# Per-head products of a recurrent mixer moved between its projections, TensorE's layer loop written out

## The reference, cut to what matters

```python
x = x + 0.5 * swiglu_ffn(rmsnorm_2(x, norm_ffn1[l]), ffn1_w_up[l], ffn1_w_down[l])
x = x + hybrid_mixer(rmsnorm_2(x, norm_mix[l]), ...)
x = x + 0.5 * swiglu_ffn(rmsnorm_2(x, norm_ffn2[l]), ffn2_w_up[l], ffn2_w_down[l])
```

```python
proj = h @ w_in
u_pool, u_lru, u_gelu, g_logits = split(proj)            # 512, 1280, 1280, 2048 columns
pooled = trailing means over 2, 4, 8, 16 tokens - u_pool # 4 groups of 128
y_pool = ((pooled @ w_grp + b_grp) * scale) @ w_pool_up  # 4 per-head products 128x128
v = causal_conv(u_lru)                                   # 4 taps, 10 heads of 128
r = sigmoid(v @ w_a + b_a); i = sigmoid(v @ w_x + b_x)   # 20 per-head products 128x128
h = scan of a * h + sqrt(1 - a*a) * i * v, a = exp(-8 * r * softplus(-lam))
y_lru = (h * gelu(u_gelu)) @ w_lru_up
out = (sigmoid(g) halves: g_pool * y_pool + g_lru * y_lru) @ w_out
```

## Time and profile before

| | us |
|---|---|
| median of three runs | 2370.72 |
| the profiled execution | 2372.06 |
| its span, first to last instruction | 2370.3 |
| TensorE matmul busy | 2053.2 (87%) |
| VectorE busy | 890.1 (38%) |
| ACT busy | 735.4 (31%) |
| GpSimd busy | 27.8 (1%) |

### The profile page before, as it was taken

One profiled execution on the slowest core, in us unless ns is written; L12 is line 12 of the kernel. 1 busy time (PEld: TensorE's weight loads), 2 busy tenths in 40 slices (PEclk: granted clock), 3 DMA queues, 4 the chain that ended last, 5 costly groups with the idle time before them and its releaser, 6 DMA issues.

```text
span 2370.3 us, 35013 instructions
## 1 busy us (share of the span) xinstructions
PE 2053.2 (87%) x14775; PEld 1616.1 (68%) x14776; DVE 890.1 (38%) x1006; ACT 735.4 (31%) x796; POOL 27.8 (1%) x27
## 2 busy tenths in 40 slices
PE   7988867777777777777699998999999999899999
PEld 5858423333333333233399998999999999899999
DVE  5452100000000000000355576775555556677555
ACT  3442100000000000000143447554434443745443
POOL 0000000000000000000000001000000000100000
PEclk8997788887787878878799999999999999999999
DMA  9756699999999999999945664465574565446554
GB/s 328 286 188 248 255 429 429 429 428 428 429 428 429 429 429 429 428 429 428 366 143 156 182 205 143 146 228 178 143 228 150 166 185 189 167 136 213 178 156 130
DMA packets 235212, 657.34 MB, mean 277 GB/s; under 512 B 6932, under 2 KB 121940, under 8 KB 210516
## 3 DMA queue, kind: packets, MB, share of 16 engines
q1 hardware_dynamic: 235092, 655.62, 72.5%
HBM read 654.54 MB, written 1.05 MB: 277 GB/s over the span
## 4 chain that ended last, share of the span: by engine, by line
issue 61%; PE 38%; DVE 0%; POOL 0%; ACT 0%; DVEq 0%; POOLq 0%; ACTq 0%
PE psum L1085 12%; PE psum L1086 12%; PE psum L1087 12%; PE psum L1109 1%; PE psum L1111 1%; PE psum L1110 1%; PE psum L1149 0%; DVE work_r L2065 0%; POOL work L694 0%; DVE work L1983 0%; ACT ring_r L1382 0%; PE psum L1191 0%; PE psum L1190 0%; PE psum L1051 0%; POOL work L695 0%
## 5 line engine op out<-in xcount | busy, mean ns | idle before, releaser
L1085 PE MATMUL psum<-work_r,ring_r 128*128 128x256 f32 x2912 | 825.2, 283 | 4.2 <-DVE work_r L2065 4.2
L1087 PE MATMUL psum<-work_r,ring_r 128*128 128x256 f32 x2912 | 824.1, 283 | 0.0
L1085 PEld LDWEIGHTS psum<-work_r,ring_r 128*128 128x128 f32 x2912 | 558.8, 192 | 5.2 <-issue 4.6
L1087 PEld LDWEIGHTS psum<-work_r,ring_r 128*128 128x128 f32 x2912 | 559.0, 192 | 0.0
L1086 PE MATMUL psum<-h_lo,ring_r 128*128 128x256 f32 x1856 | 525.2, 283 | 0.0
L1846 DVE TENSOR_TENSOR ring_r<-ring,ring_r 128x2048 fp32r<-128x2048 f32 (+2 forms) x182 | 446.1, 2483 | 175.4 <-ACT ring_r L1382 174.7
L1382 ACT CAST ring_r<-ring 128x2048 fp32r<-128x2048 f32 (+2 forms) x180 | 359.6, 2035 | 369.3 <-PE psum L1087 346.7
L1086 PEld LDWEIGHTS psum<-h_lo,ring_r 128*128 128x128 f32 x1856 | 356.3, 192 | 0.1
L1086 PE MATMUL psum<-work_r,ring_r 128*128 128x256 f32 x1056 | 299.3, 283 | 0.0
L998 PE MATMUL psum<-ring,work 128*32 128x512 f32 x1536 | 215.4, 716 | 43.3 <-DMA ring<-in_w_up_e_dram 41.5
L1020 PE MATMUL psum<-ring,work 128*32 128x512 f32 x768 | 128.5, 804 | 89.2 <-DMA ring<-in_w_down_e_dram 89.2
(11 more groups left out here) (284 smaller groups left out, 1964.6 us busy)
## 6 DMA issues: line engine op xcount, KB each, us to landing
ring<-in_w_gate_e_dram SPq DMA_DIRECT2D x64, 2048.0 KB, 12.1
ring<-in_w_down_e_dram SPq DMA_DIRECT2D x48, 2048.0 KB, 31.6
ring<-in_ffn_w_up_dram SPq DMA_DIRECT2D x41, 2048.0 KB, 8.0
ring<-in_w_up_e_dram SPq DMA_DIRECT2D x32, 2048.0 KB, 21.4
work<-in_w_up_e_dram SPq DMA_DIRECT2D x32, 2048.0 KB, 30.1
ring<-in_w_in_dram SPq DMA_DIRECT2D x26, 2048.0 KB, 8.0
ring<-in_ffn_w_down_dram SPq DMA_DIRECT2D x32, 1408.0 KB, 7.0
work<-in_w_down_e_dram SPq DMA_DIRECT2D x16, 2048.0 KB, 37.2
```

The source lines that it names most:

```text
L1085: pe.matmul(out_b, w_hi[:, k, cols], hi[:, tokens], start=(k == 0), stop=False)
L1087: mm = pe.matmul(out_b, w_lo[:, k, cols], hi[:, tokens], start=False, stop=(k == n_k - 1))
```

## The change

On TensorE the per-head products no longer stand in a row: `ra 0` to `ra 2` come between `pool 0` and `pool 1`, `ra 3`, `ra 4` and `ix 0` to `ix 3` behind `pool 1`, `ix 4` between `gelu 1` and `gelu 2`, and `pmix` behind `gelu 2`. The list of groups, and with it the banks, follows that order. ACT no longer casts `proj 4` ahead of `lru_input(4)`; its two units are cast between the gates, and all five `gelu` activations come after the tanh. VectorE makes the `lo` of `proj 4` in two pieces, one ahead of the pooled values and one behind, and empties `pmix` later. Behind the scan VectorE makes one unit of `pup`, then the pool remainder, and only then the second unit and the last two groups of `g`. TensorE's loop over the layers becomes a Python loop, so its instructions stand twice in the program; ACT, VectorE, GpSimd and SP keep their loops.

The list of groups, and TensorE's code (`recurrence_gates` and `input_gates` hold what stood in the two loops):

```diff
-    mixer += [(("pool", g), "dve") for g in range(2)]
-    mixer += [(("ra", g), "act") for g in range(5)] + [(("ix", g), "act") for g in range(5)]
-    mixer += [(("pmix", g), "dve") for g in range(2)] + [(("gelu", g), "dve") for g in range(1, 5)]
+    mixer += [(("pool", 0), "dve")] + [(("ra", g), "act") for g in range(3)] + [(("pool", 1), "dve")]
+    mixer += [(("ra", g), "act") for g in (3, 4)] + [(("ix", g), "act") for g in range(4)]
+    mixer += [(("gelu", 1), "dve"), (("ix", 4), "act"), (("gelu", 2), "dve")]
+    mixer += [(("pmix", g), "dve") for g in range(2)] + [(("gelu", g), "dve") for g in (3, 4)]
...
-            with pe.Fori(0, LAYERS) as l:
+            for l in range(LAYERS):
...
-                for q in range(2):
-                    project(("pool", q), ("proj", 0), q)
-
...
+                project(("pool", 0), ("proj", 0), 0)
+                w = tile("small", 2 * HEADS + POOLS, P)
+                for q in range(3):
+                    recurrence_gates(q)
+                project(("pool", 1), ("proj", 0), 1)
+                for q in (3, 4):
+                    recurrence_gates(q)
+                for q in range(4):
+                    input_gates(q)
+                project(("gelu", 1), ("proj", 4), 0)
+                input_gates(4)
+                project(("gelu", 2), ("proj", 4), 1)
                 pe.wait_ge(pooled_ready, l + 1)
                 for q in range(2):
                     per_head(("pmix", q), w, 2 * HEADS, pooled, (2 * q, 2 * q + 1))
-                for i in (4, 5):
-                    for q in range(2):
-                        project(("gelu", 1 + 2 * (i - 4) + q), ("proj", i), q)
+                for q in range(2):
+                    project(("gelu", 3 + q), ("proj", 5), q)
```

On ACT (`head_gates` is the old body of the loop over the gates):

```diff
-                split(("proj", 4), l)
                 lru_input(4)
-                gelu(0)
...
+                for g in range(3):
+                    head_gates("ra", rgate, lo["lru_b_a"], g)
+                split(("proj", 4), l, (0,))
+                for g in (3, 4):
+                    head_gates("ra", rgate, lo["lru_b_a"], g)
+                for g in range(4):
+                    head_gates("ix", igate, lo["lru_b_x"], g)
+                split(("proj", 4), l, (1,))
                 split(("proj", 5), l)
+                head_gates("ix", igate, lo["lru_b_x"], 4)
                 wait_emptied(("ra", 4))
...
-                gelu(1)
-                gelu(2)
                 split(("proj", 6), l)
...
-                gelu(3)
-                gelu(4)
+                for g in range(5):
+                    gelu(g)
```

On VectorE:

```diff
-                split(("proj", 4), l)
                 conv(4)
                 for g in range(2):
                     scaled(pool_u[:, 2 * g:2 * g + 2, 16:], ("pool", g))
+                split(("proj", 4), l, (0,))
...
+                split(("proj", 4), l, (1,))
+                gelu_scaled(1)
+                split(("proj", 5), l)
+                gelu_scaled(2)
...
-                split(("proj", 5), l)
-                gelu_scaled(1)
-                gelu_scaled(2)
+                gelu_scaled(3)
                 split(("proj", 6), l)
-                gelu_scaled(3)
                 gelu_scaled(4)
...
-                split(("pup", 0), l)
-                gate_scaled(6)
-                gate_scaled(7)
+                split(("pup", 0), l, (0,))
                 dve.wait_ge(pool_mix_hi_ready, l + 1)
                 dve.tensor_tensor(pool_mix_lo, pool_mix.rearrange("p c t -> p (c t)"), pool_mix_hi.bitcast(F32),
                                   ALU.subtract).then_inc(pool_mix_lo_ready, 1)
+                gate_scaled(6)
+                split(("pup", 0), l, (1,))
+                gate_scaled(7)
```

More of the change, by code:

```diff
@@ L1151, in per_head, with recurrence_gates, input_gates @@
                     mm.then_inc(group_done, 1)
-                w = tile("small", 2 * HEADS + POOLS, P)
-                for q in range(5):
+                def recurrence_gates(q):
                     pe.wait_ge(v_ready, l * 5 + (q + 1))
                     per_head(("ra", q), w, 0, v, (2 * q, 2 * q + 1))
-                for q in range(5):
+                def input_gates(q):
                     per_head(("ix", q), w, HEADS, v, (2 * q, 2 * q + 1))
+                project(("pool", 0), ("proj", 0), 0)
[10 more added lines that the diff above has]
+                project(("gelu", 2), ("proj", 4), 1)
                 pe.wait_ge(pooled_ready, l + 1)
@@ L1370, in _, with split @@
                 act.copy(y_part, two_banks[1]).then_inc(y_ready, 1)
-            def split(name, turn):
+            def split(name, turn, units=None):
                 before, in_last_layer = splits.before(name)
@@ L1380, in split @@
                 act.wait_ge(loaded[ring_plan.slot(name)], ring_plan.loaded(name, turn))
-                for unit in range(dict(splits.tiles)[name]):
+                for unit in units or range(dict(splits.tiles)[name]):
                     act.copy(hi_unit(name, unit), raw_unit(name, unit)).then_inc(hi_ready, 1)
@@ L1489, in _, with head_gates @@
                 lru_input(3)
-                split(("proj", 4), l)
                 lru_input(4)
-                gelu(0)
[L1494 to L1501, removed]
+                def head_gates(part, dst, b0, g):
+                    src = done((part, g))
+                    for b in range(2):
+                        c = 2 * g + b
+                        ins = act.activation(dst[:, c, :], src[:, S * b:S * (b + 1)], ACT.Sigmoid,
+                                             bias=lc[:, b0 + c:b0 + c + 1])
+                    ins.then_inc(emptied["act"], 1)
+                for g in range(3):
[6 more added lines that the diff above has]
+                split(("proj", 4), l, (1,))
                 split(("proj", 5), l)
+                head_gates("ix", igate, lo["lru_b_x"], 4)
                 wait_emptied(("ra", 4))
```

## The result

The changed kernel takes 2343.4 us (median of four runs, 2342.35 to 2348.47), the one before 2371.0 in the same comparison: a ratio of 0.987, 95% interval 0.9853 to 0.9888, so 27.6 us less. The profiled execution has a span of 2340.5 us where it had 2370.3. I had put the time at 2348.2, in a range of 2341 to 2357.

What follows compares the result with a forecast made beforehand. TensorE, busy 87% of the span, was taken as the bound, so only its waits and lower clock could be won. 14.0 + 5.5 + 4.3 = 23.8, less 1.3, gave 22.5 us: from 2370.7 to 2348.2, range 2341 to 2357.

Steps and rivals of the forecast that it cites:

- part A: Per-head products laid between projections on TensorE: 7.0 us a layer won, 14.0 in all.
- the new waits: TensorE waiting for VectorE's `lo` units at `gelu 2` (1.2 us) and `gelu 3` (0.8 us): 2.0 us a layer.
- changes of form: Three more switches between per-head and projection products on TensorE: 0.3 us a layer lost.
- a fall of the clock behind a new wait: TensorE at its lower clock after one of the added waits: 1.3 us taken off the gain once.
- The bound of 9.3: Waits and lower clock in the per-head stretch: at most 9.3 us a layer can be won there.
- T: Start of the last product of `pool 1` on TensorE, 1425.01 before the change; forecast times count from it.
- Part B: Pool remainder moved earlier behind the scan: 2.1 us a layer plus 1.3 of lower clock, 5.5 us won.
- Part C: TensorE's layer loop written out: 5.5 us won at the turn, less a new wait of 1.2, so 4.3.
- the first (GpSimd keeps the port through its sums): GpSimd's four window sums delay unit 0 of `proj 4`; `gelu 1` waits 3.5 us; 2354.2 us, chance 0.22.
- The second (no collision): VectorE and GpSimd never block each other, so the added waits are hidden; 2343 us, chance 0.12.
- The third, instruction fetch: TensorE's written-out layer 1 stalls eight times on fetching at new addresses, 31.6 us lost; 2379.8 us, chance 0.03.
- The fourth, the missed margin in part B: Moved pieces land badly, the 1.5 us margin behind the scan is missed in both layers; 2360 us, chance 0.08.

Runs made afterwards that it cites:

- heads_only: The changed kernel with TensorE's hardware loop and the old order behind the scan put back; 2357.0 us, ratio 0.9931.
- best: Changed kernel, both `proj 4` `lo` units before pooled values, GpSimd's product held until `gelu 2` is emptied, ACT and VectorE loops written out; 2343.9 us.
- loop_only: The kernel before with only TensorE's layer loop written out; 2367.9 us, ratio 0.9981.
- changed_again: The changed kernel itself, unaltered, run again on another chip; 2346.6 us.
- changed_third: The changed kernel itself, unaltered, run a third time on a third chip; 2345.0 us.
- lo_first: The changed kernel with both `lo` units of `proj 4` ahead of the pooled values on VectorE; 2342.5 us.

## Where the prediction failed, and what held

What failed are terms of the sum. The largest is part A's: the new waits, put at 2.0 us a layer, measured 1.27, and the 0.3 us for changes of form did not show, so that part A gave 8.0 us a layer and not 7.0. The next is the 1.3 us taken off for a fall of the clock behind a new wait; no profile of the changed kernel has one. The mechanism held: the causes, the sign and each place were as forecast. The sum was 22.5 us; the layers gave 27.1 and the time 27.6. What makes the 4.6 in the layers:

- **Part A: 7.0 a layer forecast, 8.0 measured.** The bound of 9.3 held. The new waits are 1.27 us, not 2.0. The term that was mis-sized is when `lo` units become ready: unit 1 of `proj 4` at T + 12.9 and not T + 13.5, and L703's end at T + 18.9 and not T + 19.6. The former is three small steps: the unit before it ended 0.2 us earlier, the window sums behind it took 3.45 us and not 3.7, the pooled values 1.95 and not 2.05. The latter comes from ACT. I took 0.86 us a pair of gates from the eight at 1440.52, but there TensorE set the pace: its groups, four rows of 0.215 us each, come 0.86 apart at a granted clock of 1.00. Eight further ahead in the same view, which waited for nothing, show ACT's own:

```profile
1433.35 3.03 ACT L1499 ACTIVATE work<-psum,lc 128x256 f32<-128x256 f32 x8
```

That is 0.76 a pair; in the changed kernel twelve gates, six pairs, took 4.49 us, 0.75 a pair. The 0.3 us for three more changes of form did not show: twelve per-head products in a row cost 0.44 us each, where four had read 0.46.

- **The fall of the clock: 1.3 us taken off, none came.** No wait of up to 2.2 us in the changed kernel was followed by a lower grant in the profiles taken. I had guessed one fall from one case in two, and this is the largest miss beside part A.
- **Part B: 5.5 forecast, 6.2 measured.** The waits gave 2.33 us a layer, 2.09 read as waiting and 0.24 on top (last section); the lower clock of layer 1 cost 1.5 us, not 1.3, since it lasted until 2109.2 and my window ended at 2108.3. Why the profile before has this fall at all no run tells: `heads_only` has the same two waits and no fall.
- **Part C: 4.3 forecast, 4.1 measured.** The new wait is 1.36 us (1.2 forecast) in this profile and 2.2 in two others, in which part C is worth 3.3; so of the signs, "no wait above 1.5 us" held in one profile of three. The others held: none on issue, `gelu 2` behind the pooled values, L2079 ahead of `g 7`.
- **0.7 us** came at the start of layer 0 and belongs to no part: the grant stood at 0.50 for 5.3 us from the first product on before (1185.7 to 1191.1), and for 3.7 after (1183.1 to 1186.8).

Of the rivals, the first (GpSimd keeps the port through its sums) is refuted by the unit of 2.92 us, done at 1429.4 between the first and second sum; by the prediction it would have read over 6. (The lower clock that I gave it behind a wait of 3.5 us no run shows: the waits measured are of 2.2 us and less, or of 3.7 and more.) The second (no collision) is refuted by the pair of 9.84 us; `best` shows what it would have been worth. The third, instruction fetch, is refuted by `loop_only`. The fourth, the missed margin in part B, did not happen: 1.5 us were left.

The Trainium skill, "SBUF — State Buffer", section "Who interferes with whom", says that the lock is exclusive and that the order of issue decides which of the two engines waits. The traces agree in both directions: 2.92 and 9.84 us on VectorE, 3.46 instead of 1.53 on GpSimd.

What stays open is what decides whether a wait of about 2 us brings the lower clock. Two such waits stand in each of three kernels (before, `loop_only`, `heads_only`): the grant fell behind one of two, one of two and none. The waits of 2.20 and 2.23 us at the turn of `changed_again` and `changed_third` brought none either. Open too is how part A divides: moving the products on TensorE and moving `conv(4)` ahead of the `lo` of `proj 4` (4.49 us of VectorE's time) on the other engines were never run apart, and the second alone may have taken part of the wait of 6.4 us.

## What to carry to other kernels

Where one engine bounds a stretch, count from one of its instructions to the same instruction in the other kernel: a table of a few such stretches closes to 0.1 us even where the time of a run scatters by several. When independent work is laid between dependent pieces to fill a wait, ask next which other engine's helper work is now late, and whether two engines that share a port meet there; moving one piece earlier (`lo_first`) gave nothing until the collision behind it was taken away too. A loop that is written out on the bounding engine alone hands part of its gain back to the loops of the engines that feed it, here 1.4 to 2.2 us of waiting.

## What the runs showed of the hardware that I had not expected

A wait costs TensorE more than the profile reads: removing two waits of 1.27 us together gave 1.75, and removing one of 1.36 gave 1.6, about 0.24 us each on top. The rows show where it lies. The wait is counted from the end of the row before it, which overlaps its follower's by 0.16 us when there is no wait (0.28 long against a step of 0.12, or 0.38 against 0.22 for a row of the per-head products); and the first product behind a wait has its follower 0.19 us behind it and not 0.12:

```profile
1437.27 0.36 PE L1086 MATMUL psum<-work_r,ring_r 128*128 128x256 f32 x1 [0.84 <-DVE ring_r L1861]
1437.46 0.28 PE L1087 MATMUL psum<-h_lo,ring_r 128*128 128x256 f32 x1
```

The turn of VectorE's loop costs it 5.2 us of issue in the kernel before and 5.2 to 6.1 in the changed one, more than the 3.7 to 4.2 us that TensorE's own turn showed. And a GpSimd sum that VectorE holds up reads longer in the trace by what it waited (3.46 for 1.53 us), as does the VectorE unit: neither shows the wait as idle time.
